# A two-layer hybrid encoder on one core: both layers written out, values projected ahead of keys, the engines' orders redone, one convolution tap moved to ScalarE

## The reference

```python
xn = rmsnorm(x, norm_mix)
a_q, a_k, a_v, i_q, i_k, i_w, b_q, b_k, b_v, c_q, c_k, c_v, c_f = split(xn @ w_in)
o_a = dsa_block(...)     # A: indexer scores, top-k keys, softmax over the chosen keys, rotary
o_b = sb_block(...)      # B: stick-breaking: log-sigmoids, reverse running sums, exp
o_c = fox_block(...)     # C: softmax with a bias of summed log forget gates
gate = sigmoid(xn @ w_gate)
x = x + sum_n(gate_n * (o_n @ w_branch_n)) @ w_out
h = rmsnorm(x, norm_ffn) @ w_up                     # 1024 -> 2 * 2816
g, u = split(conv_b + conv_w[0]*h[t-2] + conv_w[1]*h[t-1] + conv_w[2]*h[t])
x = x + (silu(g) * u) @ w_down
```

## Time and profile before

| | us |
|---|---|
| median of three runs (2333.74 to 2342.44) | 2341.05 |
| the profiled execution's own time | 2339.58 |
| its span in the trace | 2337.9 |
| PE busy in the span | 2204.7 (94%) |
| DVE busy | 1405.7 (60%) |
| ACT busy | 878.7 (38%) |
| POOL busy | 249.0 (11%) |
| mean granted TensorE clock, share of full speed | 0.983 |

### The profile page before, as it was taken

The page is one execution under the profiler, slowest core; times in us unless marked ns, Lnnn a source line. Parts: engine busy times, 40 slices in busy tenths (PEclk is TensorE's granted clock), DMA queues, the critical chain, the costliest instruction groups (busy, mean ns, idle before and its releaser), DMA issues.

```text
span 2337.9 us, 43604 instructions
## 1 busy us (share of the span) xinstructions
PE 2204.7 (94%) x16250; PEld 2069.6 (89%) x16266; DVE 1405.7 (60%) x2563; ACT 878.7 (38%) x1467; POOL 249.0 (11%) x185
## 2 busy tenths in 40 slices
PE   6989999999999999999999899989999999999996
PEld 6878897897898999999998789978978989999996
DVE  5537735765565763577444486267666566637864
ACT  3336422634633442222222373146155244322222
POOL 2000000000033010011410010000000421000124
PEclk9999999999999999999999899999999999999998
DMA  4121132121121222222232112211111212222222
GB/s 176 58 95 37 55 100 95 39 71 46 46 82 64 80 72 91 82 81 81 91 98 84 57 46 82 102 57 55 65 42 55 86 63 73 80 91 81 81 81 96
DMA packets 51305, 176.32 MB, mean 75 GB/s; under 512 B 6033, under 2 KB 8673, under 8 KB 51153
## 3 DMA queue, kind: packets, MB, share of 16 engines
q1 hardware_dynamic: 43344, 156.45, 20.2%
q0 software_dynamic: 3488, 12.90, 1.6%
q10 hardware_dynamic: 4320, 4.87, 0.6%
HBM read 161.30 MB, written 12.90 MB: 75 GB/s over the span
## 4 chain that ended last, share of the span: by engine, by line
PE 67%; DVE 16%; issue 7%; ACT 4%; DVEq 2%; POOL 1%; ACTq 1%; DMA 0%; SPq 0%; POOLq 0%
PE d L1192 37%; PE d L1240 12%; PE ab L1271 4%; DVE wl L718 3%; DVE cv L1145 3%; DVE hb L1130 2%; DVE cv L1142 2%; PE ab L1511 2%; PE d L1552 2%; DVE cv L1148 2%; ACT wh L454 1%; PE d L1271 1%; PE d L1442 1%; PE ab L1339 1%; ACT w L611 1%
## 5 line engine op out<-in xcount | busy, mean ns | idle before, releaser
L718 DVE TENSOR_TENSOR wl<-raw,wh 128x512 fp32r<-128x512 f32 x580 | 431.4, 760 | 626.8 <-ACT wh L454 625.3
L454 ACT ACTIVATE wh<-raw 128x512 fp32r<-128x512 f32 x580 | 355.9, 627 | 860.2 <-PE d L1192 687.1
L1192 PE MATMUL d<-xh,wh 128*128 128x288 f32 x2432 | 529.8, 299 | 41.6 <-DMA cf<-in_const 15.3
L1192 PE MATMUL d<-xh,wl 128*128 128x288 f32 x2432 | 523.9, 296 | 0.0
L1192 PE MATMUL d<-xl,wh 128*128 128x288 f32 x2432 | 523.6, 296 | 0.0
L1192 PEld LDWEIGHTS d<-xh,wh 128*128 128x128 f32 x2432 | 392.4, 190 | 51.7 <-issue 30.3
L1192 PEld LDWEIGHTS d<-xh,wl 128*128 128x128 f32 x2432 | 392.7, 190 | 0.0
L1192 PEld LDWEIGHTS d<-xl,wh 128*128 128x128 f32 x2432 | 392.3, 189 | 0.0
L1240 PE MATMUL d<-xh,wh 128*128 128x288 f32 x768 | 176.5, 311 | 26.8 <-DVE g L785 16.9
L1240 PE MATMUL d<-xl,wh 128*128 128x288 f32 x768 | 166.3, 298 | 0.0
L1240 PE MATMUL d<-xh,wl 128*128 128x288 f32 x768 | 165.9, 297 | 0.0
(11 more groups left out here) (306 smaller groups left out, 3251.4 us busy)
## 6 DMA issues: line engine op xcount, KB each, us to landing
raw<-in_w SPq DMA_DIRECT2D x290, 512.0 KB, 3.3
out_o_k<-k POOLq DMA_DIRECT2D x4, 1152.0 KB, 5.8
out_o_v<-v POOLq DMA_DIRECT2D x4, 1024.0 KB, 6.6
x<-in_xT SPq DMA_DIRECT2D x8, 288.0 KB, 6.6
out_y<-z POOLq DMA_DIRECT2D x8, 288.0 KB, 3.6
k<-in_bc_k_past ACTq DMA_DIRECT2D x4, 512.0 KB, 4.1
v<-in_bc_v_past ACTq DMA_DIRECT2D x4, 512.0 KB, 4.7
cf<-in_const SPq DMA_DIRECT2D x1, 896.0 KB, 8.2
```

Source lines behind the costliest of these rows:

```text
L454: act.activation(wh[:, c % SPLIT_SLOTS, :], raw[v_ % 2][:, (c % 2) * 512:(c % 2) * 512 + 512], ACT.Copy).then_inc(high_done, 1)
L718: dve.tensor_tensor(wl[:, c % SPLIT_SLOTS, :], raw[(c // 2) % 2][:, (c % 2) * 512:(c % 2) * 512 + 512], wh[:, c % SPLIT_SLOTS, :].bitcast( ...
L1192: ins = pe.matmul(dhalf[d % 2][half], w_, r_[:, kk, HALF * half:HALF * half + HALF], start=first and n == 0, stop=last and n == len(kks) - 1)
```

## The change

The layer loops on all engines are written out (values that were computed in registers from the layer's number are now constants; the FFN's two loops over 11 pairs stay loops, on ACT over 10 with the eleventh written behind). SP's 290 loads stand one after another, and SP issues the stores of `y` instead of POOL.

- **PE**: V's units come before K's (`U_V`, `U_K`). In B the logits of the first pair (`logits_y`, `logits_z`) stand between K1 and K2, and all eight gate blocks of the first unit behind K3; in C `scores_wide` and `scores_next` stand between K1 and K2; in A the rotary's permutes go to `ab` and lie between the queries and the gate blocks. At a layer's start IQ0 and IQ1 come earlier, and the norm takes 4 passes for 8 (POOL, at the start and the end DVE, adds all eight squares). The wait for the last pair's output moves behind the first half of the first BR unit.
- **DVE**: the first pair's steps (`sums_of`, `max_step`, `scale_step`) come between the takes of K. In C's and A's later pairs `gate_take(2p-1)` comes ahead of `scale_step(0)`, and `take_output` ahead of `scale_step(1)`.
- **FFN entry**: all eight `xl` are DVE's (three ahead of the last addition to `x`, five behind it); POOL only squares.
- **FFN pairs**: the tap with the bias (`hb*w2 + b`) moves from DVE to ACT (`tap`), and both engines' orders are redone. In `w_down` the third low part of a unit comes behind the addition to `x`.

```diff
-U_K = {B: 8, C: 32}
-U_V = {B: 12, C: 36}
+U_V = {B: 8, C: 32}
+U_K = {B: 12, C: 36}
...
-            with sp.Fori(1, (LAYERS * UNITS + 2) // 2) as pair:
-                for s in range(2):
-
-                    sp.wait_ge(low_done, 4 * pair + 2 * s - 2)
-                    sp.dma_start(raw[s][:], w[bass.ds(2 * pair + s, 1)].rearrange("a p n -> (a p) n"))\
-                      .then_inc(landed[s], 16)
+            for u in range(2, LAYERS * UNITS + 2):
+
+                sp.wait_ge(low_done, 2 * u - 2)
+                sp.dma_start(raw[u % 2][:], w[u]).then_inc(landed[u % 2], 16)
+            for j in range(KD):
+                sp.wait_ge(y_ready, j + 1)
+                sp.dma_start(y[:, j, :], z[:, j, :]).then_inc(st_y, 16)
...
+                def ffn_high(f, i, c):
+                    high_part(l * CHUNKS + f * (2 * U_HALF) + 4 * i, l * (UNITS // 2) + f * (U_HALF // 2) + i, 2 * U_UP + 4 + c)
+
+                def tap(f, i, s):
+
+                    pair, row = l * FT + f * FH + i, l * 2 * FT + f * FH + i + s * FT
+                    act.wait_ge(hb_ready, 2 * pair + s + 1)
+                    act.wait_ge(act_ready, START + pair)
+                    apart(act)
+                    act.activation(cv[:, s, :], hb[:, s, 2:T + 4], ACT.Identity, bias=pr[:, bass.ds(R_CB + row, 1)],
+                                   scale=pr[:, bass.ds(R_CW + CONV * row + 2, 1)]).then_inc(taps, 1)
+
+                def silu(f, i):
+                    act.wait_ge(conv_done, START + 2 * (l * FT + f * FH + i) + 1)
+                    act.activation(cv[:, 0, :], cv[:, 0, :], ACT.Silu).then_inc(silu_done, 1)
+
+                def round_a(f, i):
+                    act.wait_ge(act_ready, START + l * FT + f * FH + i + 1)
+                    act.activation(ah[:, bass.ds(i, 1), :].rearrange("p a n -> p (a n)"), at[:], ACT.Copy).then_inc(ah_ready, 1)
+
+                def up_pair(f, i):
+                    ffn_high(f, i, 1)
+                    tap(f, i, 0)
+                    ffn_high(f, i, 2)
+                    silu(f, i)
+                    ffn_high(f, i, 3)
+                    tap(f, i, 1)
 
...
+            def plus(l, p, s):
+                dve.wait_ge(soft, (l * PAIRS + p) * 3 + s + 1)
+                a, b = YZX[s]
+                step(dve.scalar_tensor_tensor(w1[:, a:b], slot_of(B, s), 0.0, w1[:, a:b], ALU.max, ALU.add))
+                settle()
+
+            def sums_of(l, p):
+
+                plus(l, p, 0)
+                dve.tensor_copy(hi[:, 0:1024], w1[:, 0:1024]).then_inc(sp_his, 1)
+                plus(l, p, 1)
+                step(dve.tensor_copy(hi[:, 1024:1920], w1[:, 1024:1920]))
+                settle()
+                dve.tensor_tensor(lo[:, 1024:1920], w1[:, 1024:1920], hi[:, 1024:1920].bitcast(F32), ALU.subtract).then_inc(sp_los, 1)
+
...
+                        for j in range(4):
+                            low_parts(l, 2 * U_K[m] + 2 * j + 4)
+                            take(l, D_K[m] + j, 2 * U_K[m] + 2 * j + 1, k[:, j, 0:T])
+                            low_parts(l, 2 * U_K[m] + 2 * j + 5)
+                            if j == 1 and m == C:
+                                max_step(l, m, 0, 0)
+                                max_step(l, m, 0, 1)
+                            if j == 2:
+                                if m == B:
+                                    sums_of(l, 0)
+                                else:
+                                    scale_step(l, m, 0, 0)
+                                    scale_step(l, m, 0, 1)
...
-                        max_step(1)
-                        scale_step(0)
+                        if p or m == A:
+                            if p:
+                                max_step(l, m, p, 0)
+                            low_parts(l, cg + 2)
+                            max_step(l, m, p, 1)
                         if p:
                             gate_take(l, m, 2 * p - 1)
-                        scale_step(1)
+                        if p or m == A:
+                            scale_step(l, m, p, 0)
                         low_parts(l, cg + 3)
                         if p:
                             o = take_output(l, m, p - 1)
+                        if p or m == A:
+                            scale_step(l, m, p, 1)
+                        if p:
                             if m == A:
...
+                def low_f(kk):
+                    low_x(l, 2, kk, pr[:, R_GF + l * KD + kk:R_GF + l * KD + kk + 1])
 
                 for j in range(KD):
-                    low_parts(l, 2 * U_OUT + 2 * j + (4 if j == KD - 1 else 5))
+                    low_parts(l, 2 * U_OUT + 2 * j + (3 if j == KD - 1 else 4))
                     if j == KD - 1:
-                        low_x(l, 2, 0, ffn_gain(0))
-                        low_x(l, 2, 2, ffn_gain(2))
+                        for kk in range(3):
+                            low_f(kk)
                     d = D_OUT + j
                     dve.wait_ge(chunks, chunks_done(l, 2 * U_OUT + 2 * j + 2))
                     dve.tensor_tensor(x[:, j, :], x[:, j, :], dv[d % 2], ALU.add).then_inc(dfree[d % 2], 1)
-                low_x(l, 2, 4, ffn_gain(4))
+                    if j < KD - 1:
+                        low_parts(l, 2 * U_OUT + 2 * j + 5)
                 wait_taken(dve, l, D_OUT + KD - 1)
-                square_last()
-                low_x(l, 2, 6, ffn_gain(6))
+                for kk in range(3, KD):
+                    low_f(kk)
                 low_parts(l, 2 * U_OUT + 2 * KD + 3)
...
+                def take_up(f, i, s):
+                    row = f * FH + i + s * FT
+                    dve.wait_ge(chunks, l * CHUNKS + f * (2 * U_HALF) + 4 * i + SPLIT_SLOTS + 2 * U_UP + 2 * s + 2)
+                    hv = dv[s]
+                    dve.tensor_tensor(hb[:, s, 2:514], hv[:, 0:512], rstd[:, 0:512], ALU.mult)
+                    dve.tensor_copy(hb[:, s, 514:516], pr[:, bass.ds(R_SS + 2 * (l * 2 * FT + row), 2)])
+                    dve.tensor_tensor(hb[:, s, 516:580], hv[:, 512:576], rstd[:, 512:576], ALU.mult).then_inc(hb_ready, 1)
+                    dve.tensor_tensor(conv_out[:, bass.ds(row, 1), :].rearrange("p a (b n) -> p (a b) n", n=2),
+                                      hv[:, 448:576].rearrange("p (b n) -> p b n", n=64)[:, :, 62:64],
+                                      rstd[:, 448:576].rearrange("p (b n) -> p b n", n=64)[:, :, 62:64], ALU.mult).then_inc(dfree[s], 1)
+
+                def convolve(f, i, s):
+                    pair, row = l * FT + f * FH + i, l * 2 * FT + f * FH + i + s * FT
+                    now = base[0] + in_layer + 2 * (f * FH + i) + s
+                    dve.wait_ge(taps, 2 * pair + s + 1)
+                    dve.scalar_tensor_tensor(cv[:, s, :], hb[:, s, 1:T + 3], pr[:, bass.ds(R_CW + CONV * row + 1, 1)],
+                                             cv[:, s, :], ALU.mult, ALU.add).then_inc(dve_steps, 1)
+                    dve.wait_ge(dve_steps, now + 1)
+                    dve.scalar_tensor_tensor(cv[:, s, :], hb[:, s, 0:T + 2], pr[:, bass.ds(R_CW + CONV * row, 1)],
+                                             cv[:, s, :], ALU.mult, ALU.add).then_inc(conv_done, 1)
...
-                            if s == 0:
-
-                                dve.wait_ge(act_ready, START + pair)
-                            dve.wait_ge(dve_steps, now + 1)
-                            dve.wait_ge(dfree[s], START + l * (D_USES // 2) + f * (D_HALF // 2) + i + D_UP // 2 + 1)
-                            dve.tensor_scalar(cv[:, s, :], hb[:, s, 2:T + 4], pr[:, bass.ds(R_CW + CONV * row + 2, 1)],
-                                              pr[:, bass.ds(R_CB + row, 1)], ALU.mult, ALU.add).then_inc(dve_steps, 1)
-                            dve.wait_ge(dve_steps, now + 2)
...
-                for src, of in ((0, sumsq[:]), (1, tmp[:])):
-                    if src:
-                        pe.wait_ge(last_square, count)
-                    for half in range(2):
-                        ins = pe.matmul(norm_out[half], cf[:, C_ONE:C_ONE + P], of[:, HALF * half:HALF * half + HALF],
-                                        start=src == 0, stop=src == 1)
+                for half in range(2):
+                    ins = pe.matmul(norm_out[half], cf[:, C_ONE:C_ONE + P], sumsq[:, HALF * half:HALF * half + HALF], start=True, stop=True)
...
+                pe.wait_ge(o_ready, l * 3 * PAIRS + PAIRS * m + PAIRS)
+                pe.sem_inc(dfree[1 - gate_bank(m)], HEADS)
...
+                        project_values(B)
+                        pe.wait_ge(past_b, 32 * (l + 1))
+                        project(l, U_K[B], D_K[B])
+                        project(l, U_K[B] + 1, D_K[B] + 1)
+                        pe.wait_ge(v_taken, l * 8 + 2)
+                        wait_taken(pe, l, D_Q[B] + 3)
+                        wait_taken(pe, l, D_K[B])
+                        logits_y(0)
+                        pe.wait_ge(v_taken, l * 8 + 4)
```

(27 more changed lines are left out.)

679 lines of the change are left out of this document (323 added, 356 removed).

## The result

The changed kernel takes 2197.12 us (median of four runs, 2195.33 to 2208.16) against 2337.39 for the kernel before: a ratio of 0.941, 95% interval 0.937 to 0.9449. The profiled execution took 2195.33 us.

The account below looks back on a forecast made before the run. The prediction took PE's dense work as the bound, with only its idle time and halved clock recoverable. Savings of 118.1 us less 14.4 left 103.7, giving 2237 us, with 8 in 10 between 2205 and 2275.

Parts of the forecast that it names:

- A unit at full clock costs 6.40 us: Yardstick for PE's dense work: 48 matmuls a unit, from a stretch of 552 in 73.60 us.
- Loops written out: nothing: Layer loops on all engines: constants instead of registers save nothing, since PE's queue is hidden behind matmuls.
- the front's 8 us above the forecast: Layer start, KI to B's second query: idle time and clock loss covered by earlier units, saving 9.2 us.
- The deductions, 14.4 us: Taken off the savings: 7.2 us for clock falls after new waits, 7.2 for some 24 re-ordered hand-offs.
- The new wait at K3's take: B's head: PE waits 2.5 us for K3's accumulator, whose take is queued behind DVE's chain.
- The FFN pairs: First FFN half: moving one tap from DVE to ACT lets both engines fit, saving 14.4 us.
- the `al` waits at the half ends: End of FFN halves: PE's waits of 2.6 us for the last `al` and following clock loss go, 14.0 us.
- The waits for `g`: Other pairs of C and A: taking gates ahead of the wait for ACT's exponentials saves 12.3 us.
- The heads: B's head and C's first pair: new unit order covers the first steps, saving 27.1 and 16.2 us.
- FFN entry and tail: Entry: DVE's low parts run ahead of and with the unit, 13.0 us; end: SP's stores and earlier addition, 5.9.
- The pair of durations in the forecast: FFN entry: a low part took 1.97 us beside POOL's subtraction, 0.81 beside its scaling, agreeing with the port-lock rule.
- no new waits, no new clock falls: Rival for the whole kernel: the 14.4 us taken off comes back, giving 2223 us; chance 14%.

Follow-up runs that it names:

- the added matmul: Changed kernel with one extra small identity matmul (64 columns in the first layer, 128 in the second) ahead of the second up unit: 2215.14 us.
- the FFN-pair kernel: Kernel before with its layer loops written out and the changed kernel's ACT and DVE code for the FFN pairs: 2295.70 us.
- the small matmul put in: Kernel before, layers written out, with the changed kernel's FFN pairs and one small identity matmul behind the norm's passes: 2295.30 us.

## Why the prediction was wrong

The direction and most places were right; the size was not, by about 40 us. The steps that failed:

**"A unit at full clock costs 6.40 us" was the wrong yardstick.** It came from a stretch with no gaps and clock 1.00, and I took it for PE's floor, so a faster pace stood in the sum at nothing. It is one of two paces; the other is 130.0 ns, 6.24 us a unit. In the changed kernel both FFNs run at it: 3168 matmuls a layer by 3.33 ns are 10.5 us, 21 in all, or nearly 20, since a few units of the FFN were at 130.0 before too. That is the excess of the two FFN rows of the table (23.4) nearly whole, and the added matmul took just this away (21.2 us in the chain). It isn't an effect of any edit's purpose, and as far as the forecast goes it is luck: with the pairs' code alone the pace is 133.3. The clue stood in the kernel before, where the stretch up to OUT's end already runs at 130.0; in the changed kernel that one goes at 133.3. Before and after:

```profile
648.26 68.65 PE d L1192 x528
609.79 70.41 PE d L1230 x528
```

**"Loops written out: nothing"** was worth 12.5 us by itself, some of which (the boundary, the front's idle time) the forecast had under other terms. I had looked at PE's queue alone and not at what the layer's loop does on the other engines at a boundary and in the front. Whether the front's 8 us above the forecast are of this kind is open: of the 17.2, 5.1 are three spells of half clock, and of two kernels with the same front and no loops one has none of them and the other two.

**The deductions, 14.4 us, came only in part.** The new wait at K3's take is real and in its place, but 1.3 us and not 2.5, and no fall of the clock follows. A's start idles as long as before, as forecast, but in the profiled run the clock is at half behind its wait of 2.5, from 516.0 to 522.8 us and again in the second layer: PE is busy for 9.4 us in these spells, 4.7 lost. With the tap back on DVE the same wait is there and no such spell follows. Against the terms, the table shows 6.0 us missing in its last row and 1.4 at the FFN's entry. The last row holds A's clock, and the pace again, 1.8 a layer by the two rows above; the two are more than is missing. So some 6 of the 14.4 were there, A's clock and the entry, and of the other hand-offs the table shows nothing.

**The FFN pairs: right sum, wrong carrier.** I gave the 14.4 to a tap leaving DVE. With the new order the tap's move does nothing that can be measured; with the old one it costs 33 us. What carries the term, and the `al` waits at the half ends, is DVE's order: its take is no longer queued behind a low part that waits for ACT. Busy time per pair (8.83 to 7.67) was the wrong quantity: DVE wasn't full, it stood in the wrong queue.

**The waits for `g`: right size (13.9 back when both orders are undone), half the cause.** I read that `gate_take` stood behind a wait for exponentials; the same wait was also shortened from ACT's side, and either would have done.

**The heads: right size (29.8 and 16.4), shares wrong.** Of these 46.2 us, 21 to 24 come from V's copies no longer standing ahead of the first pair, and only 9 from K2 and K3 over the soft steps. What carries the rest, 13 to 16, was not put back; the eight gate blocks in a row are the likely cover, which is argued and not shown.

**FFN entry and tail** came nearly as worked out, 11.6 for 13.0 and 5.3 for 5.9. At the entry five low parts beside POOL's square and addition read:

```profile
684.22 5.88 DVE L724 SCALAR_TENSOR_TENSOR xl<-x,pr,xh 128x576 fp32r<-128x576 f32 x5
```

5.88 us, where the three ahead of them start 0.73 apart, which would make 3.7; two of the five take 1.8 and 2.0. So POOL holds up two, which I had set aside, and PE waits 1.2 us a layer for the low parts. (The Trainium skill, "SBUF — State Buffer", section "Who interferes with whom", has the port pair locked for one of the two engines where both read SBUF in this way. The trace agrees, at 2.2 us a layer, near the 2.3 worked out by the rule. The unit runs meanwhile, so that only part of it is paid.) The pair of durations in the forecast was weaker support than it said: the low part that took 0.81 us also ran beside a POOL operation that reads SBUF, the scaling, which fits only if POOL was the one held. It took 2.23 us there and 1.73 at its shortest in that trace.

Of the rivals, none took the place of the forecast; the nearest is "no new waits, no new clock falls" (2223), which still lacked the pace.

## What to carry to other kernels

Before a saving is counted against an engine's best rate, look for stretches of the same instructions that run faster elsewhere in the trace, and use the fastest as the floor. When a take or an evacuation is late, read what stands ahead of it in its engine's list and what that waits for: here the order was worth 54 us, of which some 19 were the slower pace that came with the waits, where moving work off the engine was worth nothing, or harm. Where a change cures a wait from two sides, undo both before saying which did it.

## What was not expected of the hardware

Matmuls of one shape, at granted clock 1.00 and with no wait, run at 130.0 or at 133.3 ns, and a stretch keeps its pace for as long as it isn't broken, here over 3216 matmuls, loops and changes of operand tiles included. Behind the new entry, with nothing put in and DVE's new order, ten kernels show the fast pace in 19 of 20 FFN stretches; with a small matmul put in, or with the old entry, all eight of four kernels are slow. The same program can show either (one layer fast and one slow in one run). Runs of one kernel that lie some 10 us apart, as 2208.16 here beside 2195.33 to 2197.66, fit one layer at the slow pace, 10.8 us; no trace of such a pair of runs was taken, so that is argued and not shown. The code ahead of a stretch doesn't settle it: the stretch up to OUT's end is at 130.0 ns in both layers of the FFN-pair kernel and at 133.3 in both with the small matmul put in, although in the first layer that matmul comes behind it. In the second layer these two kernels read:

```profile
1772.60 65.53 PE d L1221 x504
1768.85 67.21 PE d L1221 x504
```

What decides the pace at a stretch's beginning stays open.
